# Gate and up products interleaved between two PSUM banks in a two-layer decoder trunk, with the first pair's row factors and weights reordered

## The reference

```python
def swiglu(x, wg, wu, wd):
    return (jax.nn.silu(x @ wg) * (x @ wu)) @ wd

    for l in range(DEPTH):
        g = norm_g[l]
        h = rmsnorm(x, g[0])
        x = x + 0.5 * rmsnorm(swiglu(h, ffn_w_gate[l, 0], ffn_w_up[l, 0], ffn_w_down[l, 0]), g[1])
        ...
        x = x + rmsnorm(y, g[3])
        h = rmsnorm(x, g[4])
        y = memory_cross_attention(h, rmsnorm(mem, mem_norm_g[l]), xa_wq[l], xa_wk[l], xa_wv[l], xa_wo[l])
        x = x + rmsnorm(y, g[5])
        h = rmsnorm(x, g[6])
        x = x + 0.5 * rmsnorm(swiglu(h, ffn_w_gate[l, 1], ffn_w_up[l, 1], ffn_w_down[l, 1]), g[7])
    return x
```

## Time and profile before

| what | us |
|---|---|
| time, median of 3 runs | 1235.69 |
| lowest and highest of them | 1234.06, 1236.98 |
| the profiled execution's own time | 1236.43 |
| its span, first to last instruction | 1234.7 |
| PE busy in the span | 1135.8 (92%) |
| DVE busy | 672.5 (54%) |
| ACT busy | 562.3 (46%) |
| POOL busy | 75.0 (6%) |
| mean granted clock of PE, share of full | 0.968 |

### The profile page before, as it was taken

One profiled execution on the slowest core, in us unless ns is written; L12 is line 12 of the kernel. 1 busy time (PEld: TensorE's weight loads), 2 busy tenths in 40 slices (PEclk: granted clock), 3 DMA queues, 4 the chain that ended last, 5 costly groups with the idle time before them and its releaser, 6 DMA issues.

```text
span 1234.7 us, 18613 instructions
## 1 busy us (share of the span) xinstructions
PE 1135.8 (92%) x7634; PEld 1042.9 (84%) x7634; DVE 672.5 (54%) x829; ACT 562.3 (46%) x794; POOL 75.0 (6%) x168
## 2 busy tenths in 40 slices
PE   4899999999879989999998999997978887999997
PEld 4899999896768889999988999996856776999997
DVE  3564555653886645544465454554565654555553
ACT  5444344535637643444354434335344654433442
POOL 2100000110021100000020000002100101000000
PEclk8999999999989989999998999998998998999999
DMA  6465554534233536555544655653153341665551
GB/s 226 137 204 174 201 181 159 176 87 140 99 119 123 168 126 218 185 172 179 194 145 161 199 184 181 204 157 99 52 160 113 119 137 52 207 202 181 186 177 69
DMA packets 144348, 193.08 MB, mean 156 GB/s; under 512 B 3270, under 2 KB 127116, under 8 KB 144284
## 3 DMA queue, kind: packets, MB, share of 16 engines
q1 hardware_dynamic: 143020, 187.93, 47.1%
q0 software_dynamic: 1264, 4.25, 1.0%
HBM read 191.12 MB, written 1.05 MB: 156 GB/s over the span
## 4 chain that ended last, share of the span: by engine, by line
PE 80%; DVE 8%; ACT 6%; DMA 2%; issue 2%; POOL 1%; SPq 0%; POOLq 0%; DVEq 0%; ACTq 0%
PE psum L754 22%; PE psum L671 15%; PE psum L673 15%; PE psum L672 15%; PE psum L907 4%; DVE w_lo L1723 2%; ACT w_hi L1172 2%; PE psum L682 2%; PE psum L684 2%; PE psum L683 2%; DVE x_state L1765 1%; ACT w_hi L1168 1%; PE psum L810 1%; DVE w_lo L1718 1%; PE psum L898 1%
## 5 line engine op out<-in xcount | busy, mean ns | idle before, releaser
L1723 DVE TENSOR_TENSOR w_lo<-raw,w_hi 128x2048 fp32r<-128x2048 f32 x162 | 371.1, 2291 | 204.5 <-ACT w_hi L1172 204.2
L671 PE MATMUL psum<-h_hi,w_hi 128*128 128x256 f32 x1568 | 449.4, 287 | 20.9 <-DVE w_lo L1723 13.8
L672 PE MATMUL psum<-h_lo,w_hi 128*128 128x256 f32 x1568 | 447.8, 286 | 0.0
L673 PE MATMUL psum<-h_hi,w_lo 128*128 128x256 f32 x1568 | 447.6, 285 | 0.0
L1172 ACT ACTIVATE w_hi<-raw 128x2048 fp32r<-128x2048 f32 x162 | 310.3, 1916 | 291.4 <-PE psum L673 142.3
L671 PEld LDWEIGHTS psum<-h_hi,w_hi 128*128 128x128 f32 x1568 | 305.4, 195 | 24.6 <-DVE w_lo L1723 15.0
L672 PEld LDWEIGHTS psum<-h_lo,w_hi 128*128 128x128 f32 x1568 | 305.4, 195 | 1.8 <-issue 0.2
L673 PEld LDWEIGHTS psum<-h_hi,w_lo 128*128 128x128 f32 x1568 | 305.2, 195 | 0.0
L754 PE MATMUL psum<-w_hi,g_both 128*128 128x512 f32 x704 | 228.6, 396 | 0.0
L754 PEld LDWEIGHTS psum<-w_hi,g_both 128*128 128x128 f32 x704 | 132.7, 189 | 30.2
L754 PE MATMUL psum<-w_lo,g_both 128*128 128x512 f32 x352 | 139.6, 396 | 0.0
(11 more groups left out here) (245 smaller groups left out, 1199.3 us busy)
## 6 DMA issues: line engine op xcount, KB each, us to landing
raw<-in_ffn_w_gate SPq DMA_DIRECT2D x44, 1024.0 KB, 5.3
raw<-in_ffn_w_up SPq DMA_DIRECT2D x44, 1024.0 KB, 5.3
raw<-in_ffn_w_down SPq DMA_DIRECT2D x44, 1024.0 KB, 4.9
raw<-in_ab_w_in SPq DMA_DIRECT2D x9, 1024.0 KB, 5.4
gain_row<-in_norm_g POOLq DMA_DIRECT2D x8, 512.0 KB, 5.7
raw<-in_xa_wk SPq DMA_DIRECT2D x4, 1024.0 KB, 5.4
raw<-in_ab_w_out SPq DMA_DIRECT2D x4, 1024.0 KB, 4.8
raw<-in_xa_wq SPq DMA_DIRECT2D x4, 1024.0 KB, 5.2
```

What stands on the lines that cost most here:

```text
L671: nc.tensor.matmul(o, wh, a_hi[:, k, :], start=(k == 0), stop=False)
L672: nc.tensor.matmul(o, wh, a_lo[:, k, :], start=False, stop=False)
L673: last = nc.tensor.matmul(o, wl, a_hi[:, k, :], start=False, stop=(k == KT - 1))
L1723: nc.vector.tensor_tensor(w_lo[:, c % RING, 0:k * n], raw[:, c % RAWS, 0:k * n], w_hi[:, c % RING, 0:k * n].bitcast(F32), ALU.subtract).th ...
```

## The change

1. *Interleaving.* A new function `gate_and_up` makes G and U of a pair together: for each output half, input slice and term there is one product into G's bank, then one into U's. It waits for both chunks' splits and for both banks first, and both banks are signalled at its end. It replaces the two calls of `feature_major` for pairs 2 to 10; pairs 0 and 1 stay in sequence. `down_tile` alternates the two halves of y in the same way. The last D product of tile 0 gives one signal (`y0_full`) where each half gave its own.
2. *Start of an FFN.* G1 and U1 are split ahead of ACT's copy of the row factors. The row factor product stands between G1 and U1. DVE's `row_scale` stands between lo(G1) and lo(U1). In FFN 0 the memory transposes stand behind U1, and their copies behind act_hi(0) and act_lo(0), ahead of the split of D0.
3. *Waits.* In the loop, hi(G p+1) waits for the down product D(p-2) that used its slot. It waited for G(p). To count this, the very first transposes add one to `down_done`.
4. *Boundaries into a mixer.* The second chunk of the second mixer (s = 5) is split ahead of the last squares on ACT, and ahead of the second input tile's low part on DVE.

```diff
+            def gate_and_up(s, p, i=0):
+
+                names = [f"{w}{s}.{p}" for w in "GU"]
+                parts = [weights(C[name], i) for name in names]
+                outs = [take(name, i) for name in names]
+                for j in range(2):
+                    for k in range(KT):
+                        o = slice(P * j, P * (j + 1))
+                        for term in range(3):
+                            for (hi, lo), out_, name in zip(parts, outs, names):
+                                last = nc.tensor.matmul(out_[:, TOK * j:TOK * (j + 1)], (hi, hi, lo)[term][:, k, o],
+                                                        (h_hi, h_lo, h_hi)[term][:, k, :],
+                                                        start=(k == 0 and term == 0), stop=(k == KT - 1 and term == 2))
+                                if (j, k, term) == (1, KT - 1, 2):
+                                    filled(name, last)
...
             def down_tile(c, t, a_hi, a_lo, first, final, i=0):
-                for half in range(2):
-                    last = down_half(c, t, half, a_hi, a_lo, first, final, i)
+
+                hi, lo = weights(c, i)
+                for k in range(2):
+                    ah, al = a_hi[:, k, P * t:P * (t + 1)], a_lo[:, k, P * t:P * (t + 1)]
+                    for a, w in ((ah, hi), (ah, lo), (al, hi)):
+                        for half in range(2):
...
-                for half in range(2):
-                    down_half(c, 0, half, a_hi, a_lo, first and len(pair) == 1, True).then_inc(y0_full, 1)
+                down_tile(c, 0, a_hi, a_lo, first and len(pair) == 1, True).then_inc(y0_full, 1)
...
                 def triple(p, i=0):
-                    feature_major(f"G{s}.{p + 1}", h_hi, h_lo, i=i)
-                    feature_major(f"U{s}.{p + 1}", h_hi, h_lo, i=i)
+                    if p:
+                        gate_and_up(s, p + 1, i)
+                    else:
+                        feature_major(f"G{s}.1", h_hi, h_lo)
+                        row_factors()
+                        feature_major(f"U{s}.1", h_hi, h_lo)
+                    if (s, p) == (0, 0):
+                        memory_transposes()
                     act_ready(p, i)
...
-                feature_major(f"G{s}.{p}", h_hi, h_lo)
-                feature_major(f"U{s}.{p}", h_hi, h_lo)
+                gate_and_up(s, p)
                 pair = [(C[f"D{s}.{q}"], g_hi[:, q % 2], g_lo[:, q % 2]) for q in (p - 1, p)]
...
-                if not isinstance(i, int):
-                    s, v = used(c - RING + (name[0] == "G"))
-                    act.wait_ge(s, v + 2 * TURN // BANKS * i)
+                if not isinstance(i, int) and name[0] == "G":
+                    act.wait_ge(down_done, n_down[c + 2] - 2 + TURN * i)
...
                     input_hi(s + 1, 0, [1])
+                    if s + 1 in MIXERS:
+                        split_to(last + 2)
                     square(f"pre{s + 1}", 0, x[:, 0, :])
...
                     silu(p, i)
                     if p:
                         hi_half(c + 1, i)
-                    else:
-                        split_to(c + 1)
                     act_hi(p, i)
+                    if (s, p) == (0, 0):
+                        mem_hi()
                     hi_half(c + 2, i)
 
-                split_to(c0 + 1)
+                split_to(c0 + 3)
                 act.wait_ge(rbc_full, FFNS[s] + 1)
                 nc.scalar.activation(rbc, psum[:, 0, 0:TOK], ACT.Copy).then_inc(rbc_done, 1)
-                if s == 0:
-                    mem_hi()
...
-                split_to(c0 + 1)
-                if s == 0:
-                    mem_lo()
+                split_to(c0 + 2)
+                row_scale(s)
+                split_to(c0 + 3)
                 dve.wait_ge(rbc_done, FFNS[s] + 1)
```

More of the change, by code:

```diff
@@ L746, in mixer_begin, with down_half @@
                             input_transposes(s, 1)
-            def down_half(c, t, half, a_hi, a_lo, first, final, i=0):
-                hi, lo = weights(c, i)
+            def down_half(c, t, half, a_hi, a_lo, first, final):
+                hi, lo = weights(c)
                 for k in range(2):
@@ L760, in down_tile @@
             def down_tile(c, t, a_hi, a_lo, first, final, i=0):
-                for half in range(2):
-                    last = down_half(c, t, half, a_hi, a_lo, first, final, i)
+                hi, lo = weights(c, i)
[3 more added lines that the diff above has]
+                        for half in range(2):
+                            last = nc.tensor.matmul(
+                                psum[:, 2 * t + half, :], a, w[:, k, 512 * half:512 * (half + 1)],
+                                start=(first and k == 0 and a is ah and w is hi),
+                                stop=(final and k == 1 and a is al))
                 return last
@@ L826, in triple, with row_factors, memory_transposes @@
                     down(C[f"D{s}.{p}"], g_hi[:, p % 2], g_lo[:, p % 2], p == 0, i)
-                begin(s)
-                feature_major(f"G{s}.0", h_hi, h_lo, gate=s)
-                feature_major(f"U{s}.0", h_hi, h_lo)
-                for t in range(NT):
-                    pe.wait_ge(rdiag_done, NT * FFNS[s] + t + 1)
-                nc.tensor.matmul(psum[:, 0, 0:TOK], ones[:, :], rdiag, start=True, stop=True).then_inc(rbc_full, 1)
-                if s == 0:
+                def row_factors():
+                    for t in range(NT):
+                        pe.wait_ge(rdiag_done, NT * FFNS[s] + t + 1)
+                    nc.tensor.matmul(psum[:, 0, 0:TOK], ones[:, :], rdiag, start=True, stop=True)\
+                        .then_inc(rbc_full, 1)
+                def memory_transposes():
                     pe.wait_ge(rbc_done, 1)
@@ L843, in ffn @@
                     last.then_inc(mem_full, 1)
+                begin(s)
+                feature_major(f"G{s}.0", h_hi, h_lo, gate=s)
+                feature_major(f"U{s}.0", h_hi, h_lo)
                 for p in range(PEEL):
@@ L1214, in square_half @@
                     if t == 0:
-                        act.wait_ge(y0_full, 2 * s + half + 1)
+                        act.wait_ge(y0_full, s + 1)
                     elif half == 0:
@@ L1794, in boundary @@
                     input_lo(s + 1, 0, [1])
+                    if s + 1 in MIXERS:
+                        split_to(last + 2)
                     input_lo(s + 1, 1)
                     split_to(last + 2 + fill)
-                    if s + 1 in FFNS:
-                        row_scale(s + 1)
             def row_scale(s):
@@ L1938, in _ @@
             split_to(1)
-            row_scale(0)
             split_to(2)
```

16 lines of the change are left out of this document (6 added, 10 removed).

## The result

| | before | after |
|---|---|---|
| time, median of 4 runs, us | 1235.83 | 1275.34 |
| lowest and highest | 1234.06, 1236.98 | 1275.11, 1277.67 |
| the profiled execution's own time | 1236.43 | 1275.11 |
| its span | 1234.7 | 1273.4 |
| PE busy | 1135.8 | 1152.8 |

The kernel after takes 1.0325 times as long (95% interval 1.0307 to 1.0343). The prediction was 1275, with 1240 to 1287 as the range.

A forecast was written before the change was run, and what follows sets the result against it. TensorE (PE) was taken to bound the kernel, busy throughout the loop. Terms 11.5 + 19.7 + 2.8 - 7.2 + 7.6 + 4.8 = +39.2 us on 1236.43 give 1275.6, less 0.7 to the median: 1275 us, range 1240 to 1287.

The forecast's parts named there:

- The loop: Loop, groups 3 to 10 of each FFN: a PE stall of 0.36 us per pair, 32 in all, +11.5 us.
- gs: DVE's gate product: in the loop, to start 0.32 us after the start of a pair's last G/U product, 0.69 long.
- PE idle 0.3 to 0.4 us: Sign for the forecast: PE idle that long ahead of every interleaved group from the third on, released by DVE's low split.
- The end: End of each FFN: PE stalls 4.9 us between D9 and D10, four times, +19.7 us.
- The clock behind the ends: Slow clock after the four new stalls at the FFN ends, 1.9 us lost behind such an idle, +7.6 us.
- The starts: FFN starts: in FFN 3, D0 4.5 us earlier but group 2 only 0.6 earlier; all four starts together +2.8 us.
- The clock at the starts: Slow clock after the new stalls at the FFN starts, between nothing and 1.9 us each, taken as 1.2, +4.8.
- The boundary: Before the second mixer: wait for weights' low half goes, 5.9 won; 0.6 comes back, slow clock 1.9 won; -7.2 us.
- Alternating banks: Interleaved G and U products: alternation gives nothing, a 256-column product stays at 0.120 us.
- Rival B: Interleaved groups: alternation does speed the product; at 0.107 us each the time is 1230, with half the effect 1252; chance 0.22.
- The single signal of the first tile: First tile's squares on ACT: one starts 0.63 us later, hidden, so nothing; if never hidden, +5 over eight boundaries.
- rival A: The sum as it stands: 1261 (no slow clock at all) to 1286 (slow at every start, signals not hidden); chance 0.70.

The follow-up runs named there:

- e8_splits_first: Kernel after, with U's weight splits in the loop moved ahead of silu (high half, ACT) and of gu (low half, DVE): 1265.48 us.
- e2_end_seq: Kernel after, with G and U one after the other in pair 10 alone: 1246.77 us.
- e3_inter_only: Kernel before, with only the interleaving of pairs 2 to 10 and the wait of hi(G) it needs: 1274.79 us.
- e10_inter_d0: Kernel after, with both halves of D0's weights split one place earlier at each FFN start, ahead of silu(0) and gu(0): 1255.87 us.
- e9_inter_boundary: Kernel before, with pairs 2 to 10 interleaved and the boundary before the second mixer changed, old order at the starts: 1267.91 us.
- e5_d9_first: Kernel after, with PE doing D9 for both token tiles (24 products, not 12) before it waits for D10: 1272.54 us.
- e1_seq: Kernel after, with G and U of every pair one after the other again, the rest of the change kept: 1219.99 us.
- e6_boundary: Kernel before, with only the first weights of the second mixer split one step earlier at the boundary before it: 1227.96 us.
- e7_seq_d0: Kernel after, with G and U of every pair one after the other and D0's weights split one place earlier at each FFN start: 1210.50 us.
- e4_down_alt: Kernel before, with only the products of a D tile alternating between its two 512-column banks: 1236.01 us.

## Why the prediction was right

**The loop.** Right in cause and in sum, 0.35 us a pair against 0.36. Its inside was slightly off. I started gs 0.32 behind s, as the earlier trace rows show it behind G's last product; but s is U's last product and G's is one earlier, so gs starts 0.20 behind s, and PE 5.94 and not 6.09. In return the first product of a group takes 0.22 after a wait and not 0.12, which I had not counted. So the sign "PE idle 0.3 to 0.4 us" is not what the timeline shows: PE idles 0.20 there, and one group in each FFN comes a further 0.2 late. e8_splits_first shows the cause.

**The end.** Right: 4.80 of idle at each end for 4.93, again by the 0.12 of gs. The rule of the Trainium skill, Perfetto Trace Analysis, section Matmuls, to rotate independent groups through banks so that evacuating one overlaps the next group's products, is borne out: interleaving kept two banks, but both came free together, and the evacuation of G lost its 5.8 us of cover.

**The clock behind the ends.** 7.4 for 7.6; e2_end_seq shows that it goes with the wait. Behind the same four waits it was 5.9 in e3_inter_only, 6.8 in e8_splits_first, 7.1 in e10_inter_d0 and 7.4 in e9_inter_boundary, so a match to 0.2 is partly luck.

**The starts.** D0 was to start 4.5 us earlier in FFN 3 and to wait there; group 2 was to stand where it stood, less 0.6. D0 came 4.05 earlier, and group 2 at 0.0. FFN 0: +4.6 for +4.7. FFN 4: -0.9 for -1.1. e10_inter_d0 shows the chain. What the prediction did not see is that this part costs time against the old order once pairs are interleaved (e9_inter_boundary), since it compared only the two ends of the change.

**The clock at the starts.** The term mis-sized: "I take 1.2 each, +4.8", with 1.9 as the most that one could cost. It was 1.4, 2.5, 2.3 and 1.4, 7.7 in all. The wait ahead of D0 (1.7 to 6.4 us) and the one ahead of group 2 (2.2 to 3.8) have only the 5.6 us of D between them, so PE idles twice; and in FFN 3 the slow stretch covers 27 products (window 485.70 to 492.50 above) and not the 20 of the earlier trace rows, since PE is not idle in it for long. In FFN 0 and 7 it is half as long, 3.4 us, and costs 1.4. That the two waits together bring the slow clock is argued, not shown. With the same starts the term was 5.7 in e2_end_seq, 5.9 in e5_d9_first and 6.0 in e8_splits_first: part of the 2.9 missing is this one execution.

**The boundary.** -9.4 in the traces for -7.2. I took the 5.9 of the wait and most of the slow stretch behind it, but the transposes of the earlier trace rows also ran at the slow clock, 1.91 us for eight where they now take 1.04, and that went too. The 2.2 more won here and the 1.2 more at the start of FFN 7 (1.4 for 0.2) offset the 2.9 of the clock and the 0.6 of FFN 3: errors of opposite sign, so that the sum of 38.7 against 39.2 is closer than its terms is luck.

**Alternating banks.** Taken as nothing, and so it is: 0.120 a product, a period of 17.12 with nothing to wait for, and D's alternation within 0.1%. Rival B is out. The figure of the Trainium skill, TensorE: Matmul & The Clock Gate, section Back-to-back issue gap (109 ns for 256 columns) is not reached in either order. That section of the Trainium skill gives it for a single gap, and says itself that it counts too little for a stream of weight loads and products when the width is small; the prediction left this out. Here each product has a weight load of its own. The measurement, 120, decides.

**The single signal of the first tile.** Taken as nothing, and so it is at the ends of the FFNs, as two of the kernels show: e1_seq has one signal, e6_boundary two, and both do G and U one after the other. From D10 to the last D product they are within 0.03 us of each other at all four ends, and over the 40 products behind it within 0.02.

**The range.** The prediction gives rival A 1261 to 1286. By its own terms it would be 1263 (1275.6 less both clock terms, 12.4) to 1283 (1.9 at every start for 1.2, and the 5 of the signals). Nothing hung on it.

## What to carry to other kernels

Two products that are consumed one after the other should end one after the other: interleaving them changed nothing on the engine that computes them and took away the time in which the first one's consumer worked. A step that is moved ahead pays only as far as what queues behind it moves too; here D0 came earlier while the load that waits for D0's split did not, and e10_inter_d0 shows the gain once that split moves as well. When a wait is cut in two, look what the granted clock does behind both pieces.

## What the runs showed of the hardware that I had not expected

- The first product after a wait costs more: 0.22 us to the next one in place of 0.12 (timeline of the loop above). The 24 products of D0 behind the wait of 0.84 us in e7_seq_d0 take 0.1 longer too, 5.72 and not 5.62. The cause is not shown.
- The granted clock fell to its 1.2 GHz level behind waits of 1.8 us (ahead of D10 in e5_d9_first) and of 2.3 us (ahead of D0 in e1_seq), not only behind one of 5 us. But it stayed at 2.4 GHz behind the same 2.3 us ahead of D0 in FFN 3 of the kernel after (the next slow stretch there begins at 485.7), behind 0.84 us in e7_seq_d0, and behind 3.25 us at the start of FFN 0 of that kernel. Behind the same 3.25 us at the same place it did fall in e10_inter_d0. The windows of D0 there, e7_seq_d0 and then e10_inter_d0:

```profile
52.99:58.68 5.69, 5.69 (x25) 4.59 (x25) 5.51 (x5) 3.61 (x4) 0.00 (x0) 1.00 0.21 51
51.54:58.76 7.22, 7.22 (x24) 5.72 (x25) 6.18 (x5) 3.59 (x4) 0.00 (x0) 0.76 0.40 121
```

  So the length of one wait does not tell whether it falls; what does is open, and no run here was made for it.
- A 512-column product costs 0.234 us whether each stationary block is used once or twice in a row (e4_down_alt).
